# Small matmuls of the heads in fewer, longer groups between weight products, in three stages of an fp32 model

## The reference

```python
def blocked_bidirectional_attention(q, k, v):        # first block: 8 heads of 96 (64 + 32 rope), v of 64
    ...
    def one_block(q_blk):                            # 128 queries against all 512 keys
        s = jnp.einsum('bqhd,bkhd->bhqk', q_blk, k).astype(jnp.float32) * scale
        p = jax.nn.softmax(s, axis=-1).astype(v.dtype)
        return jnp.einsum('bhqk,bkhd->bqhd', p, v)
...
    s = jnp.einsum('bshd,bmhd->bhsm', mq, m_k)...    # first block: 4 memory heads of 128, 256 memory rows
    p = jax.nn.softmax(s, axis=-1).astype(m_v.dtype)
    o_mem = jnp.einsum('bhsm,bmhd->bshd', p, m_v)...
...
def stick_breaking_attention(q, k, v):               # second block, layer 0: 16 heads of 64
    ...
        z = jnp.einsum('bhqd,bhkd->bhqk', q[:, :, t0:t1], k[:, :, :t1]).astype(jnp.float32) * scale
        ...
        weights = jnp.where(causal, jnp.exp(jax.nn.log_sigmoid(z) + log_between), 0.0)
        outs.append(jnp.einsum('bhqk,bhkd->bhqd', weights.astype(v.dtype), v[:, :, :t1]))
...
def hgrn2_chunk_scan(q, k, v, log_f):                # second block, layer 1: 8 heads of 128
    # S_t = diag(f_t) S_{t-1} + k_t v_t^T ; o_t = S_t^T q_t
```

## Time and profile before

| | |
|---|---|
| median of 3 runs | 1893.52 us (1892.23 to 1894.54) |
| the profiled execution, its time | 1891.87 us |
| the profiled execution, its span | 1890.1 us |
| PE busy | 1856.5 us, 98% of the span |
| DVE, ACT, POOL busy | 1038.5, 853.5, 1085.8 us |
| mean granted clock of PE | 0.996 of full speed |
| chain that ended last | PE 91%, DVE 4%, ACT 2%, POOL 1%, issue 1% |
| bytes read from HBM | 156.50 MB, 84 GB/s over the span |

### The profile page before, as it was taken

The page is one execution under the profiler, slowest core; times in us unless marked ns, Lnnn a source line. Parts: engine busy times, 40 slices in busy tenths (PEclk is TensorE's granted clock), DMA queues, the critical chain, the costliest instruction groups (busy, mean ns, idle before and its releaser), DMA issues.

```text
span 1890.1 us, 28284 instructions
## 1 busy us (share of the span) xinstructions
PE 1856.5 (98%) x10454; PEld 1569.8 (83%) x10454; DVE 1038.5 (55%) x1863; ACT 853.5 (45%) x1562; POOL 1085.8 (57%) x1321
## 2 busy tenths in 40 slices
PE   8999999999999999999999999999999999999998
PEld 6888777888888888877898899878888888999997
DVE  5648664522113377775755555385755576545552
ACT  4555455633323366664544444344434354444341
POOL 5428333445557434325788888654433278888882
PEclk9999999999999999999999999999999999999999
DMA  6214222233333312112233323333222133333331
GB/s 192 59 34 123 56 56 56 62 79 90 100 106 112 89 57 68 45 57 67 89 101 101 112 90 112 101 91 88 65 61 65 46 101 101 97 105 99 103 101 56
DMA packets 269162, 160.42 MB, mean 85 GB/s; under 512 B 6137, under 2 KB 267489, under 8 KB 268898
## 3 DMA queue, kind: packets, MB, share of 16 engines
q1 hardware_dynamic: 269026, 158.61, 29.2%
HBM read 156.50 MB, written 2.10 MB: 84 GB/s over the span
## 4 chain that ended last, share of the span: by engine, by line
PE 91%; DVE 4%; ACT 2%; POOL 1%; issue 1%; DMA 0%; ACTq 0%; SPq 0%; DVEq 0%
PE bank L259 20%; PE bank L2010 13%; PE bank L622 7%; PE bank L624 7%; PE bank L623 7%; PE bank L2655 3%; PE bank L2657 3%; PE bank L2656 3%; PE bank L1602 3%; PE bank L1604 2%; PE bank L1603 2%; PE bank L424 2%; PE bank L426 2%; PE bank L425 2%; PE bank L797 1%; POOL weight_lo L241 1%
## 5 line engine op out<-in xcount | busy, mean ns | idle before, releaser
L241 POOL TENSOR_TENSOR weight_lo<-weight_stage,weight_hi 128x256 fp32r<-128x256 f32 x1160 | 961.5, 861 | 752.8 <-ACT weight_hi L229 752.8
L229 ACT ACTIVATE weight_hi<-weight_stage 128x1024 fp32r<-128x1024 f32 (+2 forms) x303 | 309.2, 1022 | 254.1 <-PE bank L259 180.9
L622 PE MATMUL bank<-a_hi,weight_lo 128*128 128x512 f32 (+1 forms) x464 | 198.5, 428 | 1.2 <-POOL weight_lo L241 0.6
L259 PE MATMUL bank<-hidden_lo,weight_hi 128*128 128x512 f32 x512 | 199.5, 390 | 0.0
L259 PE MATMUL bank<-hidden_hi,weight_lo 128*128 128x512 f32 x512 | 199.5, 390 | 0.0
L259 PE MATMUL bank<-hidden_hi,weight_hi 128*128 128x512 f32 x512 | 199.2, 389 | 0.0
L624 PE MATMUL bank<-a_hi,weight_hi 128*128 128x512 f32 (+1 forms) x464 | 182.8, 394 | 0.0
L623 PE MATMUL bank<-a_lo_rounded,weight_hi 128*128 128x512 f32 (+1 forms) x464 | 182.6, 394 | 0.0
L1976 POOL TENSOR_TENSOR block_weight_lo<-block_weight,block_weight_hi 128x256 fp32r<-128x256 f32 x156 | 126.5, 840 | 23.0 <-ACT block_weight_hi L2145 23.0
L2360 DVE TENSOR_TENSOR x_t<-x_t,bank 128x512 f32<-128x512 f32 x128 | 82.1, 678 | 90.2 <-PE bank L259 90.2
L259 PEld LDWEIGHTS bank<-hidden_hi,weight_hi 128*128 128x128 f32 x512 | 96.1, 188 | 20.2
(11 more groups left out here) (393 smaller groups left out, 4357.6 us busy)
## 6 DMA issues: line engine op xcount, KB each, us to landing
weight_stage<-in_mlp_w SPq DMA_DIRECT2D x128, 512.0 KB, 3.8
weight_stage<-in_w_in SPq DMA_DIRECT2D x57, 512.0 KB, 3.7
weight_stage<-in_hg_w_in SPq DMA_DIRECT2D x32, 512.0 KB, 3.9
weight_stage<-in_sb_w_qkv SPq DMA_DIRECT2D x24, 512.0 KB, 3.6
weight_stage<-in_w_mkv SPq DMA_DIRECT2D x8, 512.0 KB, 3.8
weight_stage<-in_w_out SPq DMA_DIRECT2D x8, 512.0 KB, 3.8
weight_stage<-in_sb_w_o SPq DMA_DIRECT2D x8, 512.0 KB, 3.8
weight_stage<-in_hg_w_o SPq DMA_DIRECT2D x8, 512.0 KB, 3.7
```

The costliest lines, as they stand in the source:

```text
L229: act.activation(self.hi[slot][:, 0:size], self.stage[slot][:, 0:size], ACT.Copy).then_inc(self.hi_done, 1)
L241: last = pool.tensor_tensor(self.lo[slot][:, part], self.stage[slot][:, part], self.hi[slot][:, part].bitcast(F32), ALU.subtract)
L259: last = pe.matmul(out, l, r, start=n == 0, stop=n == 3 * len(pairs) - 1)
L622: pe.matmul(to, wlo, ahi(k), start=k == 0, stop=False)
```

## The change

In the convolution loop the two fills of four tiles become one of eight at the step's start, and all small matmuls of the step follow it as one run; `weigh` comes one step later. The memory heads' loop does the same with two fills of two, with `mem_weigh` one step later; the last two of them stand in the first two units of the branch products. In ACT's list the `put` of the convolution loop moves from i = 1 to i = 2; that of the memory heads stays where it was. In stick-breaking, for p < 6, both fills of three become one of six at the start of the step; `spread_k` of all pairs comes behind the fill. In the scan both fills of a level come first and both heads' scores follow.

```diff
--- before.py
+++ after.py
@@ -934,12 +934,11 @@
             mem_key_sums(MEM_HEADS - 1)
             for m in range(DOUBLES):
                 p, i = divmod(m, NT)
-                fill(conv, 2 if m == 0 else 4)
+                fill(conv, 6 if m == 0 else 8)
                 if m >= 1:
                     turn(m - 1)
                 if m + 1 < DOUBLES:
                     score(m + 1)
-                fill(conv, 4)
                 if p + 1 < PAIRS:
                     if i < 2:
                         key_spread(2 * p + 2 + i)
@@ -949,23 +948,23 @@
                     mem_key_spread(i)
                 else:
                     turn_mem_v(i - 2)
-                if m >= 1:
-                    weigh(m - 1)
+                if m >= 2:
+                    weigh(m - 2)
             gate = gates()
-            fill(gate, 2)
+            fill(gate, 4)
             turn(DOUBLES - 1)
             mem_score(0)
             mem_score(1)
-            fill(gate, 2)
-            weigh(DOUBLES - 1)
+            weigh(DOUBLES - 2)
             for n in range(ITEMS):
-                fill(gate, 2)
+                fill(gate, 4)
+                if n == 0:
+                    weigh(DOUBLES - 1)
                 mem_turn(n)
                 if n + 2 < ITEMS:
                     mem_score(n + 2)
-                fill(gate, 2)
-                if n >= 1:
-                    mem_weigh(n - 1)
+                if n >= 2:
+                    mem_weigh(n - 2)
             fill(gate, 64)
 
             for i in range(8):
@@ -973,6 +972,8 @@
                     b = kind // 2
                     if i == 0 and kind < 2:
                         pe.wait_ge(gate_done, 7 + kind)
+                    if i == 0 and kind == 0:
+                        mem_weigh(ITEMS - 2)
                     if i == 0 and kind == 1:
                         mem_weigh(ITEMS - 1)
                     u = u_mix + 6 * i + kind
@@ -1452,7 +1453,7 @@
                     high_again(2 * n + 1)
             for m in range(DOUBLES):
                 p, i = divmod(m, NT)
-                if i == 1 and p >= 1:
+                if i == 2 and p >= 1:
                     put(p - 1, 8 * p)
                 for r in range(2):
                     n = item(m, r)
@@ -1693,10 +1694,11 @@
             for m in range(M):
                 p, i = divmod(m, NT)
                 more = p + 1 < PAIRS
+                early = p + 2 < PAIRS
+                some = 6 if early else 2 if i % 2 else 1
+                fill(some)
                 if i == 2 and more:
                     spread_k(p + 1)
-                some = 3 if p + 2 < PAIRS else 2 if i % 2 else 1
-                fill(some)
                 if m >= 1:
                     turn(2 * m - 2)
                     turn(2 * m - 1)
@@ -1705,7 +1707,8 @@
                 if i % 2 and m >= 3:
                     weigh(m - 3)
                     weigh(m - 2)
-                fill(3 if some == 3 else 3 - some)
+                if not early:
+                    fill(3 - some)
                 if i == 0 and more:
                     sums(p + 1, 0)
                     sums(p + 1, 1)
@@ -2763,8 +2766,8 @@
                 pair = (2 * p, 2 * p + 1)
                 left = iter(quota(p) if p else [0] + quota(p)[1:])
                 for step in range(1, LEVELS + 1):
+                    fill(next(left) + next(left))
                     for h in pair:
-                        fill(next(left))
                         score(h, step)
                     if p >= 1:
                         if step == 1:
```

## The result

The changed kernel takes 1929.5 us in the median of four runs (1926.2 to 1929.9) against 1893.6 for the kernel before: a ratio of 1.0189 with a 95% interval of 1.0176 to 1.0202, slower by 36 us. In a second set of runs it took 1927.5 against 1892.8, 1.0191 (1.0175 to 1.0207). The forecast was slower, 1922, range 1909 to 1929: the direction was right, the size 7.5 us too small, and the median lies 0.5 us above the range.

A forecast was written before the change was run, and what follows sets the result against it. PE, busy 98% of the span, was taken as the bound. Stalls 24.7 plus clock 7.75 less merges 3.1 gave +29.3 on 1891.87, so 1921.2; the median came to 1922.8, stated as 1922 us, range 1909 to 1929.

The forecast's parts named there:

- the clock's falls: Stick-breaking: granted clock falls to 0.50 behind nearly all five stalls at the sums, 5 x 1.55 = 7.75 us.
- (f): Scan: DVE's gated q comes later, so PE stalls for p = 1 and 2; 2.3 us, 0 to 3.
- (d): Convolution loop, step 2: turn_v(2) waits for DVE's rope of head 4, 1.2 us; 0.1 for the next pair.
- merged groups: Some 78 merged pairs of small matmul groups, 0.04 us each: 3.1 us gained, 1.6 to 3.9.
- (a): Stick-breaking, p = 1 to 5: sums directly behind the turns wait for ACT's v_kept, 2.03 x 5 = 10.2 us.
- (b): Memory heads: ACT's put waits for the later mem_weigh, delaying turns after n = 5, 9 and 13; together 7.75 us.
- (c): Last convolution step: turn_mem_v(1) waits for ACT's copies of turn_mem_v(0); stall 2.4 us, 2.2 to 2.6.
- (e): Stick-breaking, first step of p = 6: second turn waits for DVE's last product; 0.8 us, 0 to 1.3.
- D: Rival: more clock falls at (b), (c) and (f), or scan's DVE late at every level; 1927 to 1936, chance 0.05.
- The rival C: Half of the stalls hidden because other engines run early after a stall; 1902 to 1911 us, chance 0.09.
- E: Rival: releasers are early, so only the merging gain shows, for instance if keep_v ran before keeps; 1890.4 us, chance 0.02.

The follow-up runs named there:

- the kernel with the weigh of the memory heads mended: Changed kernel with mem_weigh of a head's last item done in steps 4, 8 and 12, with the one before it: 1919.7 us against 1927.5.
- the first block's mending: Kernel before with only the convolution-loop and memory-head changes, plus keep_mem_v(0) before keeps, weigh before turns, heads' last mem_weigh in steps 4, 8, 12: 1893.2 us against 1892.9.
- The stick-breaking stage with the mended order: Kernel before with only the stick-breaking change, plus ACT's keep_v and next q's copies ahead of the two keeps: 1893.7 us against 1892.9, ratio 1.0000.
- the scan's part alone: Kernel before with only the scan's change, both scores of a level together: 1895.4 us, ratio 1.0012.
- gated q sooner: Kernel before with only the scan's change, plus DVE's gate_q directly behind the first head's share: 1890.9 us against 1892.9, ratio 0.9988.
- first block alone: Kernel before with only the changes in the convolution loop and memory heads: 1906.4 us, ratio 1.0068.

## Why the prediction was a little too small

The step that failed is the count of the clock's falls, 5 x 1.55 = 7.75 us in the sum: they cost 11.0. Next to it stands (f), 2.3 us for the gated q of the scan, which cost 4.1. The other waits were right to 0.3 us except (d), 1.3, which didn't come.

Term by term, for the profiled execution (1926.2, 34.3 us over that of before; the sum of the prediction was 29.3). The prediction took its stalls from start to start, so they are measured here by the starts of the same weight product in two kernels; "idle" is the wait in the rows.

| term | predicted | measured | from |
|---|---|---|---|
| merged groups | -3.1 | -3.8 | 0.045 each in the first block, 0.04 in stick-breaking, 0.06 in the scan |
| (a) sums behind the turns | 10.2 | 10.4 | 5 x 2.09, of which 1.86 idle |
| (b) memory heads' put | 7.75 | 7.9 | four waits at L836, 7.1 idle |
| (c) turn_mem_v(1) | 2.4 | 2.5 | one wait at L755, 2.32 idle |
| (d) turn_v(2), turn_v(3) | 1.3 | 0 | no wait in the row of L726 |
| (e) start of p = 6 | 0.8 | 0.9 | one wait at L1665, 0.75 idle |
| (f) scan, gated q | 2.3 | 4.1 | 3.6 idle (4.4 - 0.8) |
| falls of the clock | 7.75 | 11.0 | below |
| in no term | 0 | 0.9 | 0.7 in the convolution loop, 0.2 behind stick-breaking |

The sum is 33.9 of 34.3. The 0.7 is the difference, over the convolution loop, between the kernel with the weigh of the memory heads mended and the first block's mending, which has the loop's `weigh` ahead of `turn_v`. This accounts for 5.0 us (34.3 less 29.3) of the 7.5 that the forecast was short. The other 2.5 lie between the profiled execution and the median: the changed kernel's median is 3.3 us above its profiled execution, where the forecast went only 0.8 above its own sum (1921.2 to 1922).

**The merges** were worth a little more than was taken for them. The Trainium skill (TensorE: Matmul & The Clock Gate, Architectural detail) lets PE pull weight loads ahead of matmuls in flight; read as in the prediction, that a switch then costs nothing, the merges would be worth nothing. The stick-breaking stage with the mended order shows 0.04 us for each, the scan 0.06.

**The waits** were right in place, releaser and size but for (d), (e)'s releaser and (f)'s size: 24.7 predicted, 25.8 measured from start to start. ACT's chain behind the turns, the put that was left ahead of its weigh, the copies of the memory values and the gated q each came as worked out, and each went when the instruction that was named was moved, on ACT or DVE or in PE's weigh, with PE's merged groups left in place (1912.7 to 1893.7, 1906.4 to 1893.2). That is what shows the cause, more than the waits' rows.

**(d)** failed at "the weigh ... that stood between its cause, key_spread, and it moves behind": it does, but the rope did not follow key_spread, it came at the end of a DVE list that ran without a stop for 5 us, and that list ran faster now. Before, GpSimd made weight tiles while DVE turned a query and summed the taps, and DVE's instructions took up to 1.22 us; now GpSimd starts later and they take 0.68 and 0.75. Before (DVE, then POOL):

```profile
187.03 1.22 DVE L1047 TENSOR_TENSOR q_heads<-q_heads,cos 32x512 f32<-32x512 f32 x1
...
185.82 4.14 POOL L241 TENSOR_TENSOR weight_lo<-weight_stage,weight_hi 128x256 fp32r<-128x256 f32 x4 [8.51 <-ACT weight_hi L229]
```

Now:

```profile
185.43 0.68 DVE L1048 TENSOR_TENSOR q_heads<-q_heads,cos 32x512 f32<-32x512 f32 x1
...
187.08 3.02 POOL L241 TENSOR_TENSOR weight_lo<-weight_stage,weight_hi 128x256 fp32r<-128x256 f32 x4 [10.99 <-ACT weight_hi L229]
```

Three such instructions and a tap save 1.8 us together. The rope starts at 193.96 where it started at 196.98, and PE is there at 195.06, 0.4 behind the rope's end: without the 1.8 a stall of some 1.4 would have come, by my estimate. That GpSimd is the cause is argued from the overlap in these rows, no run tests it. **(f)** took 1.15 us for the first head's share on DVE, where its rows now take 1.99 (1382.71 to 1384.70, above), of which 1.43 reaches PE (1.84 less 0.41); and the second gated q of each pair, 0.34, was not looked at. Moving gate_q ahead of the second share and of apply removed all of it. **(e)** had its wait right (0.75 for 0.8), though the row names ACT's keep (L1851) and not DVE as its releaser; with ACT's order mended the same wait, 0.74, is put down to DVE. The 0.82 at the next turns of another step and the 0.28 at the scores behind them are not the change's: the scan's part alone has the same two with stick-breaking untouched. They stand where the fall at p = 6 doesn't come.

**The clock.** "I take a fall at nearly all of them, 5 x 1.55 = 7.75 us; ... (b) or (c) could add one or two more" had the five right, and nearly their price: 1.6 each among full products, 8.0. The Trainium skill says that activity releases the throttle (TensorE: Matmul & The Clock Gate, What's actually happening), and the 20 falls behind a wait beside narrow passes agree with it. One fall each behind (b) and (c) is what came, 3.1, as the text said it could, but they were left out of the sum. The scan's entry has one piece more, 1.5, the start of the kernel one less, -1.4. The fall of p = 6 is gone, which is worth only 0.2, for the waits that take its place. And the fall at 144.6 costs nothing: by the starts of the products the changed kernel stands 1.4 us ahead of the one before at 140 and still at 160. GpSimd is busy 3.30 of the 3.30 us there (row above), PE waits for its tiles in any case, and with the slower clock it waits less (PE's waits in the kernel before, then in the changed one):

```profile
PE bank L622 <- POOL weight_lo L241: 3.8, 5, 1.2
```

```profile
PE bank L622 <- POOL weight_lo L241: 2.1, 3, 1.2
```

So a fall has a price of its place, 1.6 where PE sets the pace and 0 to 0.2 where another engine does; the prediction had one price for all, taken at p = 6, where the fall itself cost 0.2. The runs of the changed kernel lie between 1926.2 and 1931.9 in both sets, and the clock, 0.991 to 0.987, goes with it: one or two falls more or less. The range's upper end, 1929, took in only the lower edge of D. D named 1927 to 1936 with a chance of 0.05: its number holds, its reasons hold in part, with falls at (b) and (c) but none at (f) and no lateness of DVE at every level. The number of falls isn't a fixed property of a kernel: of five profiled kernels whose stick-breaking stage is that of before, the old wait at p = 6 is followed by a fall in three (before, first block mended, gated q sooner) and by none in two (first block alone, in the odd execution with a clock of 0.95, and scan alone). A range built from one profile should have been wider by two falls on either side.

The rival C (half of the waits hidden) fell: of the waits worked out, only (d) did not come, and none of the others was shorter by more than 0.3 us a piece, which I put down to ACT and DVE losing as much time in them as PE (argued, not measured). E's condition, keep_v ahead of the keeps, is what the experiments then built; it took all of (a) away only together with the square of the next q.

The fall at 144.6 lies ahead of everything that was changed. These are PE's rows there, in the changed kernel:

```profile
140.63 0.95 PE L653 MATMUL bank<-const,scratch 96*128 96x1 f32 x8
...
143.53 0.35 PE L622 MATMUL bank<-mem_hi_rounded,weight_lo 128*128 128x256 f32 x1 [1.21 <-POOL weight_lo L241]
```

Eight one-column passes and a wait of 1.21. The kernel before has the same rows with a wait of 1.22, and its clock stays up; it fell in both profiles of the changed kernel and in the scan's part alone (142.6), and in no other. What stays open is what decides at such a place: this one, the length of the fall behind the scan's entry, p = 6, and the two of five behind a wait of 0.44 come and go between kernels that are equal up to there. No run here tells it.

## What to carry to other kernels

Products between two small matmul groups are cover for the other engines' work between them. Before merging groups, write down for each second group who releases it and when that engine could start; a group that needs what ACT or DVE make of the group just ahead must keep its products, or the releasing engine's list must be turned so that what doesn't depend on the group ahead is done first. A merged pair gave 0.04 to 0.06 us here, a wait opened by it 1.9 to 2.1 and, beside narrow passes, another 1.6 through the clock: one bad place outweighs sixty to ninety good ones. With a few steps of ACT's and DVE's lists and the weighs moved, the kernel with all but one of the same merges is 4 us faster than before (1892.9 to 1888.9).

## What the runs showed of the hardware

- A wait costs 0.17 to 0.25 us more than its idle time, in the starts behind it, even where the clock stays: 0.17 (wait of 0.44), 0.21 (2.32, before L755), 0.23 (1.86, before the sums), 0.25 (1.77, among full products).
- A wait as short as 0.44 us in the middle of sixteen two-column passes was followed by 3.4 us at half of the clock in two of five equal places; one of 1.86 us ahead of them in 20 of 20; one of 1.77 us among full products in one of five; sixteen such passes behind eight transposes without a wait in none of five.
- At a granted clock of 0.50 product starts stand about twice as far apart as at 1.00, and a fall of 3.4 us costs 1.55 to 1.6 us of time where PE sets the pace. At 144.6, where GpSimd was busy throughout, it cost nothing, and at p = 6, where DVE and ACT were next to hold PE up, 0.2. When the clock was still low as the sums came (688.9 to 699.0), it stayed low for 10 us.
- A wait of 1.73 or 1.74 us before L424 at the end of stick-breaking, among full products, was followed by a fall in three of fourteen profiles (857.4, 858.7, 861.7).
- DVE instructions of 32x512 that took 0.68 us took 1.04 to 1.22 while GpSimd worked on a weight tile (185.82 to 189.96 before the change).
- One execution of the first block's part alone had a granted clock of 0.95 from start to end outside its falls, and took 1912.0 us where its other three runs took 1905.4 to 1907.2.
